# A three-block transformer kernel in split float32: moving the start of two sets of stationary buffers by 128 and 256 bytes

## The reference

```python
x = x + conformer_conv(rms_norm(x), w_in, ...)      # w_in 2048 x 6144, w_out 2048 x 2048
x = x + hgrn2_mixer(rms_norm(x), w_in, ...)         # w_in 2048 x 10240, w_out 2048 x 2048
x = x + sliding_window_attention(rms_norm(x), ...)  # w_qkv 2048 x 2560, w_o 2048 x 2048
x = x + (silu(h @ w_gate) * (h @ w_up)) @ w_down    # h = rms_norm(x); 2048 x 5632, twice, and 5632 x 2048
```

## Time and profile before

| | |
|---|---|
| median of 3 runs | 1979.06 us (1976.77 to 1981.01) |
| profiled execution, device time | 1979.96 us |
| its span, first to last instruction | 1978.2 us |
| mean granted TensorE clock | 0.997 of full |
| TensorE matmuls busy | 1954.0 us, 99% |
| weight loads (PEld) busy | 1602.2 us, 81% |
| VectorE, ScalarE busy | 1248.0 us, 1081.2 us |
| windows of `conv_out`, `hgrn_out`, `att_out`, `down` | 93, 96, 108.5 and 240.5 us |

### The profile page before, as it was taken

How to read it: one execution, slowest core, us unless ns; L and a number is a source line. 1 busy time by engine, 2 the same in 40 slices (tenths; PEclk the granted TensorE clock), 3 DMA queues, 4 the chain that set the end, 5 groups by cost and what they waited for, 6 DMA issues and landing times.

```text
span 1978.2 us, 26935 instructions
## 1 busy us (share of the span) xinstructions
PE 1954.0 (99%) x9924; PEld 1602.2 (81%) x9924; DVE 1248.0 (63%) x1799; ACT 1081.2 (55%) x1429; POOL 220.7 (11%) x99
## 2 busy tenths in 40 slices
PE   7999999999999999999999999999999999999999
PEld 6888878888887878787887778888888888888887
DVE  5699976554868677686567885555445454444443
ACT  6444465546768585875456775544344444443332
POOL 0889840000000000000000100000000000000000
PEclk9999999999999999999999999999999999999999
DMA  8665645565545455554555445666656666656664
GB/s 295 196 189 180 188 152 191 170 204 169 162 148 169 144 166 154 154 160 154 176 183 160 137 128 160 203 191 190 192 170 192 199 187 192 189 188 194 196 192 161
DMA packets 183004, 352.45 MB, mean 178 GB/s; under 512 B 11776, under 2 KB 12288, under 8 KB 182912
## 3 DMA queue, kind: packets, MB, share of 16 engines
q1 hardware_dynamic: 181488, 350.68, 57.8%
q10 hardware_dynamic: 1424, 0.53, 0.1%
HBM read 349.07 MB, written 2.10 MB: 178 GB/s over the span
## 4 chain that ended last, share of the span: by engine, by line
PE 90%; ACT 3%; DVE 3%; issue 2%; DMA 1%; DVEq 1%; ACTq 1%; SPq 0%
PE acc L428 28%; PE acc L430 28%; PE acc L429 28%; PE T L410 2%; PE T L551 2%; ACT w_hi L707 1%; DVE w_lo L1105 1%; PE T L647 1%; PE T L636 1%; DVEq L1091 0%; DMA raw<-in_conv_w_in_dram 0%; PE T L562 0%; PE T L543 0%; PE T L561 0%; DVE Xc L1264 0%
## 5 line engine op out<-in xcount | busy, mean ns | idle before, releaser
L1105 DVE TENSOR_TENSOR w_lo<-raw,w_hi 128x1024 fp32r<-128x1024 f32 x568 | 690.0, 1223 | 641.1 <-ACT w_hi L707 633.9
L707 ACT ACTIVATE w_hi<-raw 128x1024 fp32r<-128x1024 f32 x656 | 684.4, 1058 | 525.7 <-PE acc L430 493.7
L428 PE MATMUL acc<-w_hi,h_hi 128*128 128x512 f32 x1888 | 747.2, 396 | 14.7 <-DVE w_lo L1105 14.6
L430 PE MATMUL acc<-w_hi,h_lo 128*128 128x512 f32 x1888 | 736.4, 390 | 0.0
L429 PE MATMUL acc<-w_lo,h_hi 128*128 128x512 f32 x1888 | 735.9, 390 | 0.0
L428 PEld LDWEIGHTS acc<-w_hi,h_hi 128*128 128x128 f32 x1888 | 354.9, 188 | 97.1 <-issue 14.0
L430 PEld LDWEIGHTS acc<-w_hi,h_lo 128*128 128x128 f32 x1888 | 354.8, 188 | 75.1
L429 PEld LDWEIGHTS acc<-w_lo,h_hi 128*128 128x128 f32 x1888 | 355.2, 188 | 70.5
L390 POOL TENSOR_TENSOR w_lo<-raw,w_hi 128x1024 fp32r<-128x1024 f32 x80 | 190.2, 2412 | 80.2 <-ACT w_hi L707 79.8
L1167 DVE SCALAR_TENSOR_TENSOR T<-vpad,feat,T 128x256 f32<-128x256 f32 x464 | 182.5, 485 | 0.0
L428 PE MATMUL acc<-w_hi,y_hi 128*128 128x512 f32 x384 | 154.0, 401 | 5.8 <-DVE hy_lo L1110 2.8
(11 more groups left out here) (220 smaller groups left out, 1319.6 us busy)
## 6 DMA issues: line engine op xcount, KB each, us to landing
raw<-in_hgrn_w_in_dram SPq DMA_DIRECT2D x160, 512.0 KB, 3.7
raw<-in_conv_w_in_dram SPq DMA_DIRECT2D x96, 512.0 KB, 3.9
raw<-in_ffn_w_gate_dram SPq DMA_DIRECT2D x88, 512.0 KB, 4.3
raw<-in_ffn_w_up_dram SPq DMA_DIRECT2D x88, 512.0 KB, 4.1
raw<-in_ffn_w_down_dram SPq DMA_DIRECT2D x88, 512.0 KB, 4.7
raw<-in_attn_w_qkv_dram SPq DMA_DIRECT2D x40, 512.0 KB, 3.8
raw<-in_conv_w_out_dram SPq DMA_DIRECT2D x32, 512.0 KB, 4.7
raw<-in_hgrn_w_out_dram SPq DMA_DIRECT2D x32, 512.0 KB, 4.3
```

Source lines behind the costliest of these rows:

```text
L428: nc.tensor.matmul(o, hi[:, kt, a], w_hi[:, slot, kk, :], start=kt == 0, stop=False)
L430: last = nc.tensor.matmul(o, lo[:, kt, a], w_hi[:, slot, kk, :], start=False, stop=kt == p.chunks * CK - 1)
L707: A(w_hi[:, slot, :, :], raw[:, slot, :, :], ACT.Copy).then_inc(hi_ready, 1)
L1105: TT(w_lo[:, slot, :, :], raw[:, slot, :, :], rounded(w_hi[:, slot, :, :]), ALU.subtract).then_inc(split_ready, 1)
```

## The change

The pad ahead of the turned buffers grows by 32 floats, and a new pad of 32 floats stands ahead of the feed-forward's buffers:

```diff
@@ -177,7 +177,7 @@
         rs = sb(ctx, "rs", [P, 4, TB])
         none = sb(ctx, "none", [P, 2])
         norm0 = sb(ctx, "norm0", [P, KT])
-        sb(ctx, "align_turned", [P, 40])
+        sb(ctx, "align_turned", [P, 72])
 
         mix = ExitStack()
         y_hi = sb(mix, "y_hi", [P, KT, S], F32R)
@@ -247,6 +247,7 @@
         yl2.close()
         mix.close()
 
+        sb(ctx, "align_ffn", [P, 32])
         f_hi = sb(ctx, "f_hi", [P, FKT, S], F32R)
         f_lo = sb(ctx, "f_lo", [P, FKT, S], F32R)
 
```

## The result

| | before | after |
|---|---|---|
| median of 15 runs each | 1977.96 us (1974.62 to 1981.6) | 1983.17 us (1981.04 to 1985.05) |
| ratio, 95% interval | | 1.0023 (1.0015 to 1.0030) |
| span of the profiled execution | 1978.2 us | 1979.8 us |
| mean granted TensorE clock in it | 0.997 | 0.999 |
| distance of two matmuls' starts at full clock: h / y / f | 227.2 / 227.4 / 226.7 ns | 227.2 / 232.5 / 226.7 ns |

The medians differ by 5.2 us, 0.26%; the ratio, 1.0023, makes it 4.5 us, and its interval 3.0 to 5.9 us. The forecast was no change. The last row of the table is a mean over all distances between 200 and 260 ns of a kind, from the trace's own start times; it leaves out waits, hooks and the stretches at the lower clock. Hooks between the chunks make the means of `h` and `y` a little longer than the clean 226.7.

What follows compares the result with a forecast made beforehand. TensorE bounds the kernel, by number of matmuls times distance of starts. The profiled 1979.96 us plus 0 from all three points gave 1980.0, or 1979 us as a median; range 1962 to 2000 us.

Steps and rivals of the forecast that it cites:

- no change: Whole kernel: the favoured case, time between 1975 and 1983 us, chance 0.50.
- The bound: Whole kernel: TensorE busy 1954.0 of 1978.2 us, so time is number of matmuls times distance of two starts.
- the control: Distances in gate_up, whose offset stays 0, were to stay at 226.7 ns whatever conv_out and down did.
- point 1: The 2208 weight matmuls at new offsets, 1152 at 128 and 1056 at 256: effect taken as 0.
- the rows called as witnesses: Attention value product and HGRN levels 2 and 3: equal times, 0.87 and 1.15 us, taken to show offset 256 free.
- The bounds: On the 2208 matmuls: excess gone, -13.3 ns each, -29.4 us, to excess doubled, +13.3 ns, +29.4 us.
- the excess of 13.3 ns: Each weight matmul at full clock: 226.7 ns measured over a bare stream of 213.3, the only thing offset could change.
- the prediction's own sign: Forecast wrong if weight loads stand out from 188 ns or the matmul distance moves by more than 1.8 ns.
- The sensitivities: Witness rows: a price above 1.2 ns per matmul in attention or 0.3 ns in HGRN would show.
- the slower one: The 2208 loads: tiles crossing a 512-byte line pay +13.3 ns, 29.4 us, 2008 us; slower had chance 0.27.
- one offset only: Slower rival's partial case: only one of offsets 128 and 256 pays, 14 to 15 us, 1994 us; slower 0.27 overall.
- The faster rival: Four phases: load and stream no longer meet at one place modulo 512, up to 29.4 us less, 1950 us; chance 0.23.

Runs made afterwards that it cites:

- e3: Kernel before with a 32-float pad ahead of raw: every buffer, weights too, 128 bytes higher, all offsets 0; 1979.1 us in one run.
- e5: Kernel before with only w_lo moved, 128 bytes further; 2011.89 us against 1977.14, one run each.
- e10: Kernel before with w_lo at +256, y_lo, hy_lo and f_hi at 128, y_hi and f_lo at 0; one run 1986.85 us against 1977.11.
- e7: Kernel before with 64-column stationary tiles in down, f at 0, y at 64; one run 1987.39 us against 1977.14.
- e6: Kernel before with y_hi at 16, y_lo and hy_lo at 0, f_hi and f_lo at 4; one run 1987.99 us against 1977.14.
- e1: Kernel before with y at 128 and f at 0, one half of the change; 1983.72 us against 1978.19, ratio 1.0029.
- e4: Kernel before with y_hi at 64, y_lo and hy_lo at 192, f_hi at 32, f_lo at 96; one run 1987.94 us against 1978.19.
- e12: Kernel before with y and f both at offset 256; 1978.54 us against 1977.11, ratio 1.0002.
- e11: Kernel before with w_hi and w_lo both 128 bytes further, all 7872 weight matmuls at offset 384; one run 2012.99 us against 1977.11.
- e2: Kernel before with y at 0 and f at 128; 1984.61 us, ratio 1.0035.
- e8: Kernel before with 64-column stationary tiles in down, f at 128, y at 384; one run 1985.67 us against 1977.14.

## Why the prediction was wrong

- **The bound was right.** TensorE's distances carry the time, and the loss came through them whole: 5.8 to 6.5 us by the distances, 3.0 to 5.9 us by the interval. `gate_up` served as the control, and stayed at 226.7 ns.
- **The step that failed** is point 1: "I take 0", on the ground that the moving read passes every place modulo 512 four times, so that "the offset shifts the moment more than the number of meetings". At offset 128 the distance is 232.3 ns and not 226.7: what the argument put at nothing, where the two reads begin relative to each other, has a price. That 0 came out right for offset 256 was luck: the argument treats 128 and 256 alike, and the rows called as witnesses run at a rate at which no price shows (next point). The price hardly depends on how large the offset is, 4 bytes cost as much as 128. The bounds held, but the excess of 13.3 ns was not the size: the price is 5.6 ns, and 1152 of the 2208 matmuls pay it. By the prediction's own sign, a distance that moves by more than 1.8 ns, the forecast was wrong.
- **The rows used as witnesses run at a rate at which no price shows.** The earlier trace rows try a difference of 256 between small tiles of unrounded float32, and their equality was true and remains so. The prediction said "they speak for offset 256 and only by likeness" and then let them carry offset 128 too. The likeness fails as well: the transposes with `ident` are such small tiles at offset 128, and they keep their 109 ns. That is 109 / 128 = 0.85 ns for each column, where the weight products have 226.7 / 512 = 0.44 at full clock and 426.7 / 512 = 0.83 at the lower one, at which they show no price either. In the earlier trace rows the longer steps between starts are 209 ns for 256 columns, 0.82 ns for each, as slow as the lower level. The sensitivities were too fine, too: the starts in the earlier trace rows come in pairs 6 or 7 ns apart, so there are 4 and 16 steps and not 8 and 32, and the rows could show 2.5 and 0.6 ns per step. The 1152 matmuls at 128 had no witness, and should have been priced between the two ends on their own.
- **The rival that came true in its direction is the slower one**, at "one offset only", with 5.2 us where it had 14 to 15, and its mechanism is refuted: a tile at offset 4 crosses a 512-byte border of the weights' grid by 4 bytes, one at 256 by half, and only the former pays. The border isn't what counts; in every run with 128 stationary columns the distance was at its base where all starts were equal modulo 256, and longer in the mean where they were not. The faster rival (the two reads start together at the same place and so collide) has it the wrong way round: the same place modulo 256 is the best that was tried.
- **The ports.** The Trainium skill (SBUF — State Buffer, "Who interferes with whom") gives TensorE two independent read ports, one for the moving operand and one for weight loads. The prediction took from it that "the offset is worth exactly 0", and there the trace disagrees: 226.7 ns with the operands at one place, 232.1 with the same operands 128 bytes apart, and 226.7 again when both are moved (e3). That the ports share something is what this suggests, not what a run has shown.
- **Points 2 and 3** held: the run with offset 256 at both places moved every work buffer by 256 bytes and the change by 128, and neither shows anything outside the distances. The transposes, whose offset to `ident` was new, kept their 109 ns. One reading of rows was loose: a 9 in the clock row stands for 90% or more, and the earlier trace rows has 0.97 and 0.98 in two windows, so the clock was not full in every slice.

What stays open: why one stream of three at another place slows all three (e5), why two loads off cost more than three (e10), why half-size loads lengthen the distance (e7), and what the 13.3 ns are. Open, too, is why the same places give two rates in different stretches of one execution: 226.7 and 233.3 ns for y in e6, 232.3 and 233.3 for y in e1, where the distances repeat every seven matmuls in the one kind, as after the change, and alternate between 229 and 238 in the other. That the offset causes the loss is shown; by what mechanism is not.

## What to carry to other kernels

Where a float32r product streams 512 columns with a weight load beside each matmul, let all operands of the stream, moving and stationary, begin at the same place modulo 256 bytes in a partition. Small tensors ahead of them (an odd row of statistics, an epsilon) break this silently: 32 bytes, the unit to which this program rounds its buffers, cost as much as 128 (e4), and a slice that begins 4 bytes into a buffer does too (e6). A pad takes some bytes and no time (e12), and with all 7872 weight products 128 off the program loses 36 us of 1977 (e11). When a trace holds a witness for one value of a size, ask it for that value only, and see first that it runs at the rate of what it is to stand for.

## What the runs showed of the hardware

- With both weight buffers at one place modulo 256 and all stationary tiles off it, the price is 5 to 6 ns on a distance of 226.7 ns, at full clock (e1, e2, e6, e7, e8, e11). At the lower level, 1.2 GHz, there is none: the seven distances with `y` at 128 in e1 are 425 to 428 ns and the six in e11 426 or 427, as the 426.7 of the earlier trace rows. Two lines of e1 stand below: 2.99 us / 7 = 427.1 ns.
- The transposes of unrounded float32 (128 columns, 109 ns apart) show no price at an offset of 128, at full clock (before against after).
- The place is relative and its period is 256 bytes, for loads (e12, offsets 128, 384 and 256) and for streams (e10 against e5).
- One of the two weight buffers at 128 (w_lo alone, e5) cost 35 us, 4.4 ns for each of 7872 matmuls, nearly as much as both (e11, 36 us). One stationary operand of three at 128 (y_lo or hy_lo, e10) cost 3.8 ns for each matmul of its phases, where all three cost 5.1.
- With operands at different places the distance can take either of two values from one uninterrupted stretch to the next: 226.7 or 233.3 ns for `y` in e6.
- Weight loads of 64 columns in place of 128 lengthened the distance from 226.7 to 230.0 ns at offset 0, though a load took 135 ns and not 188 (e7).

```profile
905.96 0.63 PE L430 MATMUL acc<-w_lo,y_hi 128*128 128x512 f32 x1
...
908.95 0.48 PE L431 MATMUL acc<-w_hi,hy_lo 128*128 128x512 f32 x1
```
